# Values of the matrix memory: two half-depth units of 512 columns, and a rounding moved to head 6

## What is computed

```python
px = modulate(rms_norm_2(x, g_pre_mix), sh_m, sc_m) @ w_in        # 256 tokens
pc = modulate(rms_norm_2(ctx, g_pre_mix), csh_m, csc_m) @ w_in    # 256 context tokens
aqx, akx, avx, mqx, mkx, mvx, mox, mgx = jnp.split(px, SPLIT_AT, axis=-1)
# mv: the memory's values, 4 heads x 128 = 512 columns, for the context and for the tokens
h_ml_c, st_f, st_b = mlstm_bidir(cq, ck, cv, cg, zero, zero)
h_ml_x, _, _ = mlstm_bidir(xq, xk, xv, xg, st_f, st_b)
ml_x = mlstm_output(h_ml_x, mox, g_mlstm_out)                     # mox: the output gate
mix_x = jnp.concatenate([att_x, ml_x], axis=-1) @ w_out
```

## Time and profile before

| | |
|---|---|
| median of three runs | 1376.34 us (1374.07 to 1376.88) |
| the profiled execution | 1376.54 us |
| its span, first to last instruction | 1374.7 us |
| TensorE busy | 1351.4 us (98%) |
| VectorE busy | 970.7 us (71%) |
| ScalarE busy | 725.6 us (53%) |
| mean granted clock of TensorE | 0.995 |

### The profile page before, as it was taken

The page is one execution under the profiler, slowest core; times in us unless marked ns, Lnnn a source line. Parts: engine busy times, 40 slices in busy tenths (PEclk is TensorE's granted clock), DMA queues, the critical chain, the costliest instruction groups (busy, mean ns, idle before and its releaser), DMA issues.

```text
span 1374.7 us, 18895 instructions
## 1 busy us (share of the span) xinstructions
PE 1351.4 (98%) x7725; PEld 1168.8 (85%) x7725; DVE 970.7 (71%) x1134; ACT 725.6 (53%) x978; POOL 121.9 (9%) x173
## 2 busy tenths in 40 slices
PE   7999999999999999999999999999999999999998
PEld 7888889878888888888888889888888868888887
DVE  6788876966786777677776867566567775765554
ACT  6444457544544446444455765544455456644443
POOL 2100000300000000000015112000013002100000
PEclk9999999999999999999999999999999999999999
DMA  9877645423877656877655427555544213365551
GB/s 294 292 252 249 210 138 184 154 92 114 316 253 259 222 183 225 289 260 263 206 170 185 154 93 234 194 192 184 179 135 126 47 34 108 105 215 196 198 187 62
DMA packets 166836, 256.13 MB, mean 186 GB/s; under 512 B 4883, under 2 KB 135230, under 8 KB 163550
## 3 DMA queue, kind: packets, MB, share of 16 engines
q1 hardware_dynamic: 164414, 248.63, 54.1%
q0 software_dynamic: 2176, 6.24, 1.7%
q10 hardware_dynamic: 160, 0.05, 0.0%
HBM read 253.59 MB, written 1.32 MB: 185 GB/s over the span
## 4 chain that ended last, share of the span: by engine, by line
PE 74%; DVE 6%; ACT 3%; POOL 2%; issue 1%; DVEq 0%; POOLq 0%; ACTq 0%
PE acc L224 22%; PE banks L617 20%; PE banks L627 11%; PE banks L186 2%; PE banks L187 2%; PE banks L188 2%; PE banks L577 2%; DVE w_lo L177 2%; ACT w_hi L171 1%; PE banks L1035 1%; PE banks L607 1%; POOL rstd L1467 1%; DVE arena L874 1%; POOL mean_sq L1464 1%; PE acc L1123 1%
## 5 line engine op out<-in xcount | busy, mean ns | idle before, releaser
L177 DVE TENSOR_TENSOR w_lo<-w_raw,w_hi 128x2048 fp32r<-128x2048 f32 x212 | 486.8, 2298 | 119.7 <-ACT w_hi L171 118.9
L171 ACT ACTIVATE w_hi<-w_raw 128x2048 fp32r<-128x2048 f32 x212 | 405.0, 1910 | 59.9 <-PE banks L188 15.3
L617 PE MATMUL banks<-h_both,w_hi 128*128 128x512 f32 x1520 | 370.6, 391 | 0.0
L617 PEld LDWEIGHTS banks<-h_both,w_hi 128*128 128x128 f32 x1520 | 278.8, 188 | 53.5 <-issue 0.9
L627 PEld LDWEIGHTS banks<-h_both,w_lo 128*128 128x128 f32 x1520 | 194.9, 191 | 7.4
L627 PE MATMUL banks<-h_both,w_lo 128*128 128x256 f32 x1520 | 197.2, 283 | 0.0
L224 PE MATMUL acc<-w_lo,act_hi 128*128 128x512 f32 x400 | 155.9, 390 | 0.0
L224 PE MATMUL acc<-w_hi,act_hi 128*128 128x512 f32 x400 | 155.8, 390 | 0.0
L224 PE MATMUL acc<-w_hi,act_lo 128*128 128x512 f32 x400 | 155.8, 390 | 0.0
L471 ACT ACTIVATE silu_gate<-banks 128x512 f32<-128x512 f32 x55 | 33.1, 601 | 155.9 <-PE banks L617 139.2
L485 ACT ACTIVATE act_hi<-act 128x512 fp32r<-128x512 f32 x50 | 31.5, 631 | 138.7 <-PE acc L224 138.7
(11 more groups left out here) (352 smaller groups left out, 2014.6 us busy)
## 6 DMA issues: line engine op xcount, KB each, us to landing
w_raw<-in_ffn_w_gu SPq DMA_DIRECT2D x88, 1024.0 KB, 5.2
w_raw<-in_ffn_w_down SPq DMA_DIRECT2D x44, 1024.0 KB, 4.9
arena<-in_w_ada SPq DMA_DIRECT2D x24, 1024.0 KB, 5.9
w_raw<-in_w_ffn_in SPq DMA_DIRECT2D x22, 1024.0 KB, 5.0
w_raw<-in_gla_w_in SPq DMA_DIRECT2D x12, 1024.0 KB, 5.3
w_raw<-in_diff_w_in SPq DMA_DIRECT2D x12, 1024.0 KB, 5.1
w_raw<-in_w_ffn_out SPq DMA_DIRECT2D x11, 1024.0 KB, 4.9
w_raw<-in_w_in SPq DMA_DIRECT2D x9, 1024.0 KB, 5.2
```

The source lines that it names most:

```text
L171: eng.activation(w_hi[:, slot, :], w_raw[:, slot, :], ACT.Copy).then_inc(sem("unit_hi"), 1)
L177: eng.tensor_tensor(w_lo[:, slot, :], w_raw[:, slot, :], w_hi[:, slot, :].bitcast(F32), ALU.subtract).then_inc(sem("unit_split"), 1)
L617: return pe.matmul(outs[ct], hi[:, k, ct * P:(ct + 1) * P], h_both[:, k, :, t], start=k == 0, stop=k == KT - 1)
```

## The change

The two units of the values are cut the other way: each holds half of the depth (4 of 8 tiles) and all 512 columns. Piece n is now one tile of 128 tokens (n // 2) by one half of the depth (n % 2), with 512 columns; the odd piece adds to the even piece's sums in the same bank. mv0 to mv3 are copied at the same places, each now one tile of 128 tokens with 512 columns. Unit 6 is last used by piece 6 and unit 7 by piece 7. The rounding of unit 9, which needs unit 6's slot, moves from head 2 to head 6, ahead of mv3.

```diff
@@ mix_sync
             for n, c in enumerate(MIX_COL):
-                load_unit(sp, u + n, w[:, :, c:c + (P if n == MIX_GATES else UC)])
+                deep = 4 * (n - MIX_MV)
+                if n in (MIX_MV, MIX_MV + 1):
+                    load_unit(sp, u + n, w[:, deep:deep + 4, MIX_COL[MIX_MV]:MIX_COL[MIX_MV] + 2 * UC])
+                else:
+                    load_unit(sp, u + n, w[:, :, c:c + (P if n == MIX_GATES else UC)])
@@ mix_scalar, values(pair)
-                if pair % 2:
-                    eng.wait_ge(sem("unit_used"), u + MIX_MV + pair // 2 + 1)
+                if pair == 3:
+                    eng.wait_ge(sem("unit_used"), u + MIX_MV + 2)
                 else:
-                    eng.wait_ge(sem("ml_pair"), pair // 2 + 1)
-                tiles, c = 2 * (pair % 2), (pair // 2) * UC
-                keep(f"mv{pair}", ml_v[:, tiles:tiles + 2, c:c + UC], halves_of(bank[3][:, :]))
+                    eng.wait_ge(sem("ml_pair"), pair + 1)
+                keep(f"mv{pair}", ml_v[:, pair, :], bank[3][:, :])
@@ mix_scalar, the heads
+                if h == 6:
+                    split_hi(eng, u + 9)
                 if h % 2 == 0:
                     values(h // 2)
-                if h == 2:
-                    split_hi(eng, u + 9)
                 if h == 6:
                     split_hi(eng, u + 10)
@@ mix_tensor, value_tile(n)
-                last = natural_columns(pe, u + MIX_MV + n // 4, [bank[3][:, (n % 2) * UC:(n % 2 + 1) * UC]], (n % 4) * P)
-                if n % 4 == 3:
+                deep, v = n % 2, u + MIX_MV + n % 2
+                pe.wait_ge(sem("unit_split"), v + 1)
+                hi, lo = (t[:, v % RING, :].rearrange("p (k c) -> p k c", k=4) for t in (w_hi, w_lo))
+                r = slice((n // 2) * P, (n // 2 + 1) * P)
+                for k in range(4):
+                    last = product(pe, bank[3][:, :], (h_hi[:, 4 * deep + k, r], h_lo[:, 4 * deep + k, r]),
+                                   (hi[:, k, :], lo[:, k, :]), deep + k == 0, deep + k == 4)
+                if n >= 6:
                     last.then_inc(sem("unit_used"), 1)
-                elif n % 4 == 1:
+                elif deep:
                     last.then_inc(sem("ml_pair"), 1)
```

## The result

| | before | after |
|---|---|---|
| median | 1376.36 us (20 runs, 1373.95 to 1378.85) | 1383.63 us (20 runs, 1374.98 to 1384.6) |
| profiled execution | 1376.54 us | 1381.92 us |
| its span | 1374.7 us | 1380.1 us |
| mean granted clock | 0.995 | 0.991 |

The ratio is 1.0039, with a 95% interval of 1.0028 to 1.005: slower by about 0.4%, and the medians are 7.3 us apart. The runs after the change are of two kinds: 5 of 20 lie between 1374.98 and 1377.70, 15 between 1381.92 and 1384.6. Before, all 20 lie under 1379. The ratios further down leave out two runs far from all others, one of 1484 us in e4 and one of 2438 us in e5, with mean granted clocks of 0.848 and 0.762.

The account below looks back on a forecast made before the run. TensorE was taken to bound the kernel, with 74% of the chain. Shorter pieces save 7 x 0.143 + 0.095 = 1.10 us, everything else nothing, so 1376.34 us becomes 1375.2; range 1373.0 to 1377.3 us.

Parts of the forecast that it names:

- The pieces: Value matmuls in attention heads 0 to 7: seven pieces shorter by 0.143 us, piece 1 by 0.095, together 1.10 us.
- the extra of the first matmul: First matmul behind transposes or scores: 0.10 us over the spacing at 256 columns, 0.09 at 512, taken as equal.
- The rounding: Unit 9's 1.90 us on ScalarE, moved to head 6, fits into 3.28 us of idling: cost nothing, 1.9 us without cover.
- the unit order: Unit 7 wanted at piece 1, unit 6 free at piece 6: subtraction done in time, only unit 9's rounding waits.
- the loads: Two 1 MB loads with runs growing from 1 to 2 KB: landing changes by at most 0.1 us, no cost.
- Rival 1: Head 0's 3.4 us low clock stretch changes: gone gives 1373.5 us, doubled 1376.9; chance 0.06 each.
- the last sign of being wrong: Last listed sign against the forecast: a low clock anywhere but near 1068 us, in head 0; no size given.
- The collision in head 6: Unit 9's rounding delays head 7's copies: 2.5 us slower, 1377.7 us, or 1379.4 with the clock falling; chance 0.08.
- Head 3: Head 3's copy was held by the rounding and comes up to 1.9 us earlier: 1373.3 us; chance 0.06.
- Closer matmuls: 512-column matmuls in the pieces overlap to 0.131 us each, saving 10.4 us: 1366 us; chance 0.02.

Follow-up runs that it names:

- e4: Changed kernel with the third part of the first output gate issued ahead of the memory's scores of head 1: 1375.69 us median, ratio 0.9994.
- e5: Changed kernel with one more low-order matmul left out in each odd piece, 0.91 us less work: 1374.03 us, ratio 0.9983.
- e1: Kernel before with only the rounding of unit 9 moved from head 2 to head 6: 1375.36 us median, ratio 0.9997.
- e8: Changed kernel with piece 1 ahead of head 0's transposes and the third gate part ahead of the memory's scores of head 1: 1373.87 us, ratio 0.9983.
- e10: Changed kernel again with piece 1 ahead of head 0's transposes and the third gate part ahead of the memory's head 1 scores: 1373.75 us, ratio 0.998.

## Why the prediction was wrong

**The pieces: right in sign and mechanism, too large by 0.3 us.** The forecast had 1.10 us, the trace 0.79. The spacing of 0.227 held (0.228 in piece 2). The sum took the extra of the first matmul as equal at both widths; piece 2 gains 0.12 us and piece 7 only 0.08 (2.92 us before, 2.84 after), for 0.143 in the sum.

**The rounding, the unit order, the loads: right.** TensorE's two waits are the same to a tenth. The subtraction of unit 9 waits 1.56 us, and head 7's copy on VectorE follows it at once; the delay is no more than the tenths that the forecast allowed, and TensorE does not wait for it. ScalarE has 1.25 us left ahead of mv3, within the 0.4 to 1.4 of the forecast. The rounding alone cost nothing (e1). The loads from w_in land in 5.3 us, where the earlier trace rows have 5.1, and TensorE waits for none of them.

**The step that failed is what lies behind it.** The sum let 1.1 us pass through the memory's heads to the end, since the earlier trace rows show TensorE at 60.30 of 60.30 with a clock of 1.00 there. That row says that the clock did not fall in one execution; it does not say how near it was. Two facts were on the table. The clock had fallen in head 0 behind light work; and the masks and scores behind 1114 are light work too. Rival 1 named the fall and let it go, or double from 3.4 to 6.8 us, in head 0. It did not ask whether a shift of one microsecond could make the clock fall elsewhere, nor for how long; only the last sign of being wrong, "a low clock anywhere but near 1068", has it, without a price. So the sum put the memory's heads at no change. There the clock stays down for 20.5 us and costs 9.0, eleven times the measured gain of 0.79.

**The rivals.** The collision in head 6 was the slower case, with 1377.7 to 1379.4 us; its sign is the measured one, its place and its mechanism are not. Head 3 was not held: e1 takes the rounding away there, and from the first scores to the attention's last values it takes 50.72 us (1061.26 to 1111.98) where the kernel before takes 50.74. Closer matmuls are out at a spacing of 0.228. The range of 1373.0 to 1377.3 holds three of the five runs under 1379, with 1377.49 and 1377.70 at its edge; for the median it is 6 us short.

**What stays open:** what the clock wants in order to stay up; whether it is the few rows, the few weight loads or something else in the light stretch that lets it fall; what holds the program to nearly the same place against the clock; and why a fall there lasts six times as long as the one in head 0. The runs show the place and the work behind which the clock falls, not the rule. The Trainium skill (TensorE: Matmul & The Clock Gate, What's actually happening) says that recent activity of TensorE decides the clock, in windows that run free of the kernel. A fall that depends on the place fits that; a place that stays the same within 0.6 us in eight profiles does not follow from it. No run here can show the windows themselves.

## What to carry to other kernels

A change that shortens work ahead of a light stretch of TensorE should be costed with the clock falling in that stretch; a granted clock of 1.00 in one profile is no proof against it. When a kernel's runs split into two groups, compare the granted clock by windows before looking for a wait; then shift the old kernel by the same time, and shift the new one back. What helped here was dense work moved into the light stretch, with no instruction added: the order of two calls took the changed kernel from 1383.63 to 1375.69 us (e4), and with piece 1 early as well to 1373.8 (e8, e10).

## What the runs showed of the hardware that was not expected

- The clock falls while TensorE is 2.00 of 2.00 us busy, and waits for nobody. The Trainium skill (TensorE: Matmul & The Clock Gate, Why this matters for your kernels) warns of idle gaps between bursts of matmuls; here the rows show none, only matmuls on 40 and 64 rows for the most part. The measurement decides: a full busy row, which is modelled, is no protection.
- Once down, it stayed down for 20.5 us, through further masks, scores, transposes and short dense parts, though the same instructions left it up in the kernel before.
- The program meets the clock at nearly the same place each time. In eight profiles whose first scores lie up to 3.1 us apart, the fall of 3.4 us in head 0 begins within 0.6 us of the same place in the program.
- A shift of 0.35 us lies between a profile with the 20.5 us fall (42.19 us behind head 0's) and one without it (42.54).
